# A two-layer MLA, HGRN2 and PEER block: the target tokens x lie by tokens from the end of their first pass on, and parts of the HGRN phase are moved

## Chip, core and metric

The kernel runs on one core of a Trainium2 chip. What is measured is the device time of the launch in microseconds: of the execution, from the first instruction to the last. A time before is the median of three runs; the profile is that of one more execution.

## What is computed

Two layers work on 256 target tokens x and 256 context tokens, each token with 1024 features, all in fp32. Layer 0 has an MLA and convolution mixer and a PEER feed-forward, for both kinds of tokens. Layer 1 has an HGRN2 mixer and a PEER feed-forward, for x alone. The result is a root-mean-square norm of x. Cut to what the change touches:

```python
x = x + mod[5] * peer_ffn(modulate(rms_norm(x, norm2_g[0]), mod[3], mod[4]), ...)   # layer 0
h = modulate(rms_norm(x, norm1_g[1]), mod[0], mod[1])                               # layer 1
q, zf, zb, i, g = split(h @ w_in)
o = gla_chunked(q, kf, i, lf, sc_f) + flip(gla_chunked(flip(q), flip(kb), ...))     # 8 heads, 4 chunks of 64
y = (rms_norm(o, 1) * norm_g * silu(g)) @ w_out
x = x + mod[2] * y
h2 = modulate(rms_norm(x, norm2_g[1]), mod[3], mod[4])
x = x + mod[5] * peer_ffn(h2, ...)
return rms_norm(x, final_norm_g)

def peer_ffn(h, ...):      # 8 heads, 128 keys a half, the best 16 of 16 x 16 sums: 16 experts of 16384
    act = gelu(einsum('nd,nhkd->nhk', h, u[eidx]))
    return einsum('nhk,nhkd->nd', softmax(top_s) * act, v[eidx])
```

## The kernel before

Activations lie transposed: `xT` has the 128 features of a tile on the partitions, 8 tiles, and the 512 tokens (x, then context) in the free dimension. Weights come as tiles of 512 KB through `wring`, a ring of four: `load_tile` (L99) lets SyncE issue tile g once the product of tile g-4 is counted in `acc_ready`. `lin` (L95) lists the products in order, `lin_matmuls` (L118) and `lin_evac` (L133) run one.

**The PEER phase** (`peer_phase`, L891) is a program by picks. A step is one head for one block of 128 tokens, it has 16 picks, and a pick is one expert per token: GpSimd gathers for it 128 rows of u and v (8 KB each, 1 MB) into one of eight slots `uv` (L1032), VectorE forms the dot products with the tokens' own rows `H2` (L1340), ScalarE gelu, gate and a diagonal (L1170, L1174, L1180), and TensorE adds diagonal times v into `pY` (L1120), two matmuls of 128x512, each of them two records. A slot is free for gather n+8 once pick n is added. In layer 0 the picks k = 4, 9 and 13 of each step from pick 148 on are added by VectorE into `Y` instead (`on_vector`, L926; L1301). The choice of experts for a step (`topk`, L1201) runs on VectorE two steps ahead. Layer 0 has 512 picks: 16 steps for the context tokens, then 16 for x. Layer 1 has 256. Beside the picks of layer 0 two companions work, `TargetMixer` (layer 0's mixer for x) and `ContextStates` (the HGRN states that the context leaves, the last of them at pick 503); each has methods `sync`, `tensor`, `scalar` and `vector` that are called with the pick's number.

**The end of a block of tokens**: `take` (L1282) copies `pY` (L1290), or adds it to `Y` (L1288), `turn_back` (L1069) transposes it to features in two halves through `pt` (L1077), and `residual` (L1309) adds it, times the modulation, into `xT` (L1316). For the first block of a pass this runs beside the next step's picks (k = 8 to 15), for the last block behind the last pick.

**A norm** (`norm_phase`, L164) is a phase of its own, with barriers about it: ScalarE squares 8 tiles (L196), TensorE sums them over the features with a matrix of ones (L207), VectorE and ScalarE form the inverse root for all columns (L213, L198, L215), VectorE multiplies (L218), and both apply gain and shift (L186, L190). It runs ahead of the HGRN phase (`n1`), ahead of layer 1's PEER phase (`np1`) and for the result (`nf`), which is then stored in one transfer of 1 MB (L285).

**The HGRN phase** (`hgrn_phase`, L2095) has three parts. First the products `hg_zz` (16 tiles, gates), values of features 0 to 511 with `wi`, `hg_qg` (16 tiles, queries and output gate), and the other values. SyncE issues `wi` (2 MB, L2143) ahead of tile 4 of `hg_zz`. GpSimd issues eight tiles of the modulation's weights `ada_w` (2 MB each, L2154), two at once and each further one when the one before last is used up; VectorE multiplies them in between the gates of the 16 half heads (L2229, L2230, `products(3 * i, 3 * i + 3)`), and TensorE sums four columns of partial results (`turn(n)`, L2158) after tiles 5, 8, 11 and 14 of `hg_zz` and 0, 4 and 8 of `hg_qg`, and the last time behind the values.

```python
L2227  for i in range(2 * HEADS):
L2228      lin_done(dve, 5, i + 1)
L2229      chain(v.tensor_scalar(F[:, i], F[:, i], room[:, i:i + 1], low[:, i:i + 1], ALU.mult, ALU.add))
L2230      chain(v.tensor_scalar(KK[:, i], F[:, i], -1.0, 1.0, ALU.mult, ALU.add))
L2231      products(3 * i, 3 * i + 3)
```

Second the recurrence, head by head: exponentials on ScalarE two heads ahead (L2274), their products on VectorE (L2308) and GpSimd (L2270), key transposes, intra-chunk scores, states and output on TensorE, and ScalarE's copy of a head's output (L2301), which releases the output bank for the next. Third the output: squares of all heads (L2423), their column sums (L2453), an inverse root, 16 diagonals (L2437) that TensorE spreads over the features (L2460), the products with norm, gain and gate (L2441, L2444), then `hg_out` (8 tiles, each the features of one output tile, L127), which waits for all eight heads, and a residual per tile (L230). Behind it stand `np1` and the opening of `peer_phase`: queries and scores of head 0 for 256 tokens, the tokens' own rows (L1087, L1151), head 1; then `topk` and the first gather. SyncE loads the 12 query tiles that the ring does not hold into `held` at the start of this phase (L1009).

## Time and profile before

| | |
|---|---|
| three runs | 2677.03, 2678.91, 2681.13 us; median 2678.91 |
| the profiled execution | 2672.03 us, its span 2669.9 us |
| TensorE busy | 2259.8 us, 85% |
| VectorE busy | 1813.7 us, 68% |
| ScalarE busy | 1113.0 us, 42% |
| GpSimd busy | 895.4 us, 34% |
| DMA | 949.67 MB, mean 356 GB/s over the span |
| mean granted clock of TensorE | 0.958 of full speed |

The times of rows are microseconds from the start of the span. PE is TensorE's matmuls, PEld its weight loads, DVE VectorE, ACT ScalarE, POOL GpSimd, SP SyncE. A timeline row merges instructions of one line that follow each other ("x16"); its second number reaches from the start of the first to the end of the last. In brackets stands how long the engine had been idle and what ended that.

### The profile page before, as it was taken

The numbers are of one execution on the slowest core, as the hardware profiler recorded it, in microseconds if no ns is written. First come the engines' busy times: TensorE is split into PE (matmuls) and PEld (weight loads), VectorE is DVE, ScalarE is ACT, GpSimd is POOL, SyncE is SP. The second block draws the span as 40 slices with busy tenths as digits, with TensorE's granted clock in tenths as the row PEclk, the third lists the DMA queues.
The fourth block names the chain that finished last, engine by engine and source line by source line (L and its number), as shares of the span: only waits on it lengthen the run. The fifth ranks groups of instructions, "written<-read, shape, count | busy, mean of one in ns | idle before, by whom it ended". The sixth has DMA issues, their size and how long they took to land. (4 is left out here: it accounts for less than half of the span.)

```text
span 2669.9 us, 24714 instructions
## 1 busy us (share of the span) xinstructions
PE 2259.8 (85%) x7264; PEld 1239.9 (46%) x7264; DVE 1813.7 (68%) x4325; ACT 1113.0 (42%) x3039; POOL 895.4 (34%) x802
## 2 busy tenths in 40 slices
PE   7999799999887988888888877699787888888776
PEld 3776445543453324444444443477663333333222
DVE  3745988876668666868687867571637666666655
ACT  1352558754535343434343434211314444444443
POOL 0000444443344434444444444000204444444431
PEclk8999899999899999899999999899998999999999
DMA  8423999999999999999999999584049999999995
GB/s 324 158 87 105 367 418 419 406 421 420 397 418 420 420 420 419 415 419 414 418 412 420 414 417 411 210 308 136 1 163 409 427 427 427 426 427 427 426 427 230
DMA packets 146247, 949.67 MB, mean 356 GB/s; under 512 B 16448, under 2 KB 22080, under 8 KB 43712
## 3 DMA queue, kind: packets, MB, share of 16 engines
q0 software_dynamic: 112608, 834.72, 75.4%
q1 hardware_dynamic: 33504, 113.37, 11.6%
q8 instruction: 58, 0.95, 0.1%
q14 instruction: 77, 0.63, 0.1%
HBM read 946.98 MB, written 1.05 MB: 355 GB/s over the span
## 5 line engine op out<-in xcount | busy, mean ns | idle before, releaser
L1120 PE MATMUL pY<-uv,diag 128*128 128x512 f32 x2796 | 1369.5, 625 | 306.3 <-ACT diag L1180 304.5
L1032 POOL DMA_INDIRECT uv<-uv_dram,idx x768 | 869.9, 1133 | 1321.3 <-PE pY L1120 826.0
L1340 DVE SCALAR_TENSOR_TENSOR uv<-uv,H 128x1024 f32<-128x1024 f32 x768 | 940.3, 1224 | 534.1 <-DMA uv<-uv_dram,idx 532.0
L1120 PEld LDWEIGHTS pY<-uv,diag 128*128 128x128 f32 x2796 | 511.9, 195 | 1043.6 <-ACT diag L1180 572.0
L1170 ACT ACTIVATE gelu<-dots 128x1 f32<-128x1 f32 x768 | 155.1, 202 | 979.7 <-DVE uv L1340 978.6
L1180 ACT ACTIVATE diag<-cst,coef 128x128 f32<-128x128 f32 x699 | 280.6, 401 | 65.7 <-ACT coef L1174 1.9
L1174 ACT ACTIVATE coef<-gelu,gate 128x1 f32<-128x1 f32 x768 | 226.3, 295 | 28.1 <-ACT gelu L1170 0.4
L1055 PE MATMUL pqs<-h2T,wring 128*128 128x256 f32 x576 | 133.5, 387 | 11.3 <-PEq L168 7.4
L1055 PEld LDWEIGHTS pqs<-h2T,wring 128*128 128x128 f32 x576 | 111.8, 195 | 39.4 <-issue 25.1
L127 PE MATMUL plh<-h1T,wring 128*128 128x256 f32 x512 | 117.5, 391 | 11.8 <-PEq L168 7.4
L127 PEld LDWEIGHTS plh<-h1T,wring 128*128 128x128 f32 x512 | 99.9, 197 | 27.1 <-issue 8.2
L461 PE MATMUL f_pl<-h,wring 128*128 128x256 f32 x384 | 95.8, 394 | 1.3 <-ACT h L619 1.3
L1170 ACT ACT_TABLE_LOAD x72 | 92.4, 1283 | 1.3
L1301 DVE SCALAR_TENSOR_TENSOR Y<-uv,coef,Y 128x1024 f32<-128x1024 f32 x65 | 83.3, 1281 | 0.0
L461 PEld LDWEIGHTS f_pl<-h,wring 128*128 128x128 f32 x384 | 73.4, 198 | 11.4 <-issue 1.8
L1907 PE MATMUL side<-h2T,arena 128*128 128x256 f32 x256 | 63.4, 392 | 0.0
L1340 DVE DVE_READ_ACCUMULATOR uv<-uv,H 128x1 f32 x768 | 63.3, 82 | 0.0
L1907 PEld LDWEIGHTS side<-h2T,arena 128*128 128x128 f32 x256 | 51.2, 200 | 21.1 <-issue 15.2
L1144 ACT ACT_TABLE_LOAD x46 | 59.0, 1283 | 0.8
L1758 DVE SCALAR_TENSOR_TENSOR arena<-arena,convw 128x256 f32<-128x256 f32 x120 | 56.8, 473 | 0.3
L798 DVE SCALAR_TENSOR_TENSOR convc<-gatedc,convw,convc 128x256 f32<-128x256 f32 x120 | 48.9, 482 | 0.0
L752 DVE SCALAR_TENSOR_TENSOR mod_part<-aw,scT,mod_part 128x512 f32<-128x512 f32 x70 | 47.0, 745 | 0.4
...
## 6 DMA issues: line engine op xcount, KB each, us to landing
...
uv<-uv_dram,idx POOLq DMA_INDIRECT x768, 14.8
...
```

The source lines that it names most:

```text
L127: last = nc.tensor.matmul(psum[:, j, 0:n_cols], wring[:, j, k * P:(k + 1) * P], rhs(k), start=(k == 0), stop=(k == KT - 1))
L461: last = mm(pl[g // 2 % 2][:, i % 2, :], wring[:, g % RING, k * P:(k + 1) * P], rhs, start=(k == 0 and (i % 2 == 0 or not (seq == 2 and i ...
L1032: nc.gpsimd.indirect_dma_start(out=uv[:, n % SLOTS, :], out_offset=None, in_=t[f"uv{l}"], in_offset=bass.IndirectOffsetOnAxis(ap=idx[:, s ...
L1055: last = nc.tensor.matmul(pq[:, i, :], w[:, k * P:(k + 1) * P], hT[:, k, own:own + T], start=(k == 0), stop=(k == KT - 1))
L1120: last = nc.tensor.matmul(pY[:, b, half * 512:(half + 1) * 512], diag[:, multiplied(n) % DIAGS, :], uv[:, n % SLOTS, D + half * 512:D + (h ...
L1144: nc.scalar.activation(gate[:, s % KEPT, :], gate[:, s % KEPT, :], ACT.Exp, bias=nmax[:, s:s + 1], accum_out=den[:, s:s + 1]).then_inc(s_e ...
L1170: nc.scalar.activation(gelu[:, r:r + 1], dots[:, s % 2, k:k + 1], ACT.Gelu).then_inc(s_gelu, 1)
L1174: nc.scalar.activation(coef[:, r:r + 1], gelu[:, r:r + 1], ACT.Copy, scale=gate[:, s % KEPT, k:k + 1]).then_inc(s_coef, 1)
L1180: nc.scalar.activation(diag[:, m % DIAGS, :], ident, ACT.Copy, scale=coef[:, r:r + 1]).then_inc(s_diag, 1)
L1301: last = v.scalar_tensor_tensor(out=to, in0=row, scalar=coef[:, r:r + 1], in1=to, op0=ALU.mult, op1=ALU.add)
L1340: v.scalar_tensor_tensor(out=uv[:, j, 0:D], in0=uv[:, j, 0:D], scalar=1.0, in1=H2[:, own, :], op0=ALU.mult, op1=ALU.mult, accum_out=dots[: ...
L1907: last = mm(to, self.ring[:, i % 3, k * P:(k + 1) * P], self.hT[:, k, :], start=(k == 0), stop=(k == KT - 1), skip_group_check=True)
```

## The change

All parts stand in one change.

- x by tokens. At the end of x's PEER pass in layer 0 `RowFinish` takes the place of `take`, `turn_back` and `residual` for x, and of the norm `n1`. Rows of x and of the modulation are made ahead, beside the picks. For each block of 128 tokens VectorE multiplies the sum by the gate and adds x (`RowNorm.sums`), ScalarE squares with a row sum, the inverse root is one number per token, and TensorE turns the block to features by matmuls with the diagonal of these numbers, so that it is normed on the way (`turn`); gain and shift are applied on the way out of PSUM. Block 0 runs beside the last picks, from pick 499 on, block 1 behind the last. `xT` holds x by tokens from there on.
- The last two steps of layer 0 add nothing on VectorE, and what it had added before is folded into the rows of x in the step before the last.
- The same class ends layer 1: it makes the result by rows and stores it in four transfers of 256 KB; the norm `nf` and the one store are gone. The host lays the output out accordingly.
- The HGRN output and the opening of layer 1 are one program inside the PEER phase (`RowOutput`): the product with `hg_out` has tokens on its output rows and sums over heads, tile by tile (each tile now holds the rows of one head), so it can begin when the first head is gated; block 0 is finished, normed, turned and asked for its experts ahead of block 1. `np1` is gone. The squares of the recurrence's output are made per head, ahead of the output's copy.
- The HGRN phase: SyncE issues tiles 4 to 9 of `hg_zz` ahead of `wi`; GpSimd waits for the fourth tile's product before it issues `ada_w`; its memsets, the exponentials and products of heads 0 and 1 stand in the first part, ahead of the last values' copies; `turn(7)` stands ahead of the last values.
- `Y` and one `hT` are made once for the whole kernel.

The diff's core (indentation reduced):

```diff
   s, k = divmod(n, TOPK)
-  return l == 0 and n >= VECTOR_FROM and k in (4, 9, 13)
+  return l == 0 and n >= VECTOR_FROM and k in (4, 9, 13) and s < steps - 2
...
       residual(done, 1)
-   take(steps - 1)
-   residual(steps - 1, 0)
-   residual(steps - 1, 1)
+   for n in TAIL:
+    for side in sides:
+     side.vector(dve, n)
+class RowNorm:
...
+ def sums(self, dve, b):
+  v = self.nc.vector
+  for h in range(2):
+   own = slice(2 * h, 2 * h + 2)
+   v.tensor_tensor(self.temp(b)[:, own], self.src(b)[:, own], self.gate[:, own], ALU.mult).then_inc(self.prod, 1)
+  for h in range(2):
+   own = slice(2 * h, 2 * h + 2)
+   dve.wait_ge(self.prod, 2 * b + h + 1)
+   v.tensor_tensor(self.out(b)[:, own], self.temp(b)[:, own], self.residual(b)[:, own], ALU.add).then_inc(self.x, 1)
+ def squares(self, act, b):
+  for h in range(2):
+   own = slice(2 * h, 2 * h + 2)
+   act.wait_ge(self.x, 2 * b + h + 1)
+   self.nc.scalar.activation(self.junk(b)[:, own], self.out(b)[:, own], ACT.Square,
+         accum_out=self.ss[:, 2 * b + h:2 * b + h + 1]).then_inc(self.sq, 1)
+ def mean(self, dve, b):
+  v, ms = self.nc.vector, self.ms[:, b:b + 1]
+  dve.wait_ge(self.sq, 2 * b + 2)
+  v.tensor_tensor(ms, self.ss[:, 2 * b:2 * b + 1], self.ss[:, 2 * b + 1:2 * b + 2], ALU.add).then_inc(self.mean_ready, 1)
+  dve.wait_ge(self.mean_ready, 2 * b + 1)
+  v.tensor_scalar(ms, ms, 1.0 / D, EPS, ALU.mult, ALU.add).then_inc(self.mean_ready, 1)
+ def root(self, act, b):
+  act.wait_ge(self.mean_ready, 2 * b + 2)
+  self.nc.scalar.activation(self.ms[:, b:b + 1], self.ms[:, b:b + 1], ACT.Sqrt).then_inc(self.root_ready, 1)
+ def inverse(self, dve, b):
+  dve.wait_ge(self.root_ready, b + 1)
+  self.nc.vector.reciprocal(self.ms[:, b:b + 1], self.ms[:, b:b + 1]).then_inc(self.inv, 1)
+  dve.wait_ge(self.inv, b + 1)
+ def diagonal(self, dve, b):
+  self.nc.vector.tensor_scalar(self.spread(b), self.ident, self.ms[:, b:b + 1], None, ALU.mult).then_inc(self.diag, 1)
+ def turn(self, pe, b, banks):
+  pe.wait_ge(self.diag, b + 1)
+  for k in range(KT):
+   last = self.nc.tensor.matmul(banks[k // 4][:, k % 4 * P:(k % 4 + 1) * P], self.out_cols(b, k), self.spread(b),
+          start=True, stop=True)
+   if k % 4 == 3:
+    last.then_inc(self.turned, 1)
+ def affine(self, eng, b, k, banks, to, gain, shift):
+  eng.wait_ge(self.turned, 2 * b + k // 4 + 1)
+  own = banks[k // 4][:, k % 4 * P:(k % 4 + 1) * P]
+  if eng is self.nc.scalar:
+   eng.activation(to, own, ACT.Identity, scale=gain, bias=shift).then_inc(self.h_act, 1)
+  else:
+   eng.tensor_scalar(to, own, gain, shift, ALU.mult, ALU.add).then_inc(self.h_dve, 1)
+def feature_rows(nc, bank, half, column, ident):
+ for k in range(4):
+  last = nc.tensor.matmul(bank[:, k * P:(k + 1) * P], column(4 * half + k).broadcast_to([P, P]), ident,
+        start=True, stop=True)
+ return last
+class RowFinish:
+ TAIL = 12
+ SUM, SQUARE, MEAN, ROOT, INVERSE, TURN, AFFINE = 0, 1, 2, 2, 3, 4, 5
+ OPEN, GATE, ADDED = 317, 467, (2, 4, 6, 8)
...
+ def begins(self, b):
+  return self.picks - TOPK + 3 if b == 0 else self.picks
...
+ def tensor(self, pe, n):
...
+      pe.wait_ge(self.g_copied, 1)
+     feature_rows(nc, self.banks[0], half, self.column(0), self.ident).then_inc(self.g_rows, 1)
+   for b in range(2):
+    if n == self.begins(b) + self.TURN:
+     if b == 0:
+      pe.wait_ge(self.context.k_copied, 8)
+      pe.wait_ge(self.context.st, 16)
+     else:
+      pe.wait_ge(row.h_act, 4)
+      pe.wait_ge(row.h_dve, 4)
+     row.turn(pe, b, self.banks)
...
+   if n == self.begins(b) + self.SQUARE:
+    row.squares(act, b)
+   if n == self.begins(b) + self.ROOT:
+    row.root(act, b)
+   if self.l == 0 and n == self.begins(b) + self.AFFINE:
+    for k in range(4):
+     row.affine(act, b, k, self.banks, *self.into(b, k))
...
+  for b in range(2):
+   if n == self.begins(b) + self.SUM:
+    dve.wait_ge(self.s_pick, self.own_picks[b])
+    if b == 0:
+     dve.wait_ge(self.g_copied, 2 if self.l == 0 else 4)
+     if self.l == 0:
+      dve.wait_ge(self.copied, 4)
+      if self.added:
+       dve.wait_ge(self.folded, 4)
+    row.sums(dve, b)
+   if n == self.begins(b) + self.MEAN:
+    row.mean(dve, b)
+   if n == self.begins(b) + self.INVERSE:
+    row.inverse(dve, b)
+    if self.l == 0:
+     row.diagonal(dve, b)
+    else:
+     for h in range(2):
+      own = slice(2 * h, 2 * h + 2)
+      v.scalar_tensor_tensor(out=row.temp(b)[:, own], in0=row.out(b)[:, own], scalar=row.ms[:, b:b + 1],
+           in1=self.rows["gain"][:, own], op0=ALU.mult, op1=ALU.mult).then_inc(self.y, 1)
+   if self.l == 0 and n == self.begins(b) + self.AFFINE:
+    for k in range(4, KT):
+     row.affine(dve, b, k, self.banks, *self.into(b, k))
+ def sync(self, sp, n):
+  if self.l == 1:
+   for b in range(2):
+    for h in range(2):
+     if n == self.begins(b) + self.INVERSE:
+      sp.wait_ge(self.y, 2 * b + h + 1)
+      sp.dma_start(self.final[1][:, b, h * 512:(h + 1) * 512],
+         self.row.temp(b)[:, 2 * h:2 * h + 2].rearrange("p j n -> p (j n)")).then_inc(self.final[2], 16)
+class RowOutput:
...
+ def sync_out(self, sp):
+  for i in range(RING, KT):
+   self.load_tile(sp, "hg_out", i, self.out_first + i)
+  for i in range(RING):
+   self.load_tile(sp, "peer_q1", i, self.q_first + i)
...
+  for half in range(2):
+   last = feature_rows(nc, self.pY[:, 0, half * 512:(half + 1) * 512], half, lambda k: self.modT[:, 1, 2, k, 0:1], self.ident)
+  last.then_inc(self.g_rows, 1)
+  for n in range(HEADS * M):
+   last = mm(self.pt[:, n:n + 1], self.sq[:, n // M, (n % M) * P:(n % M + 1) * P], self.ones[:, 0:1], start=True, stop=True)
+  last.then_inc(self.r_sum, 1)
+  def wide(q):
+   pe.wait_ge(self.r_diag, q + 1)
+   if q >= 3:
+    pe.wait_ge(self.r_on, q - 2)
+   mm(self.wide[q % 3], self.ones[:], self.diag[:, 2 * M * q:2 * M * (q + 1)].rearrange("p m n -> p (m n)"),
+   start=True, stop=True).then_inc(self.r_wide, 1)
+  def product(k, blocks):
+   g = self.out_first + k
+   pe.wait_ge(self.w_loaded[g % RING], 16 * (g // RING + 1))
+   pe.wait_ge(self.r_gated, k + 1)
+   if k == 0:
+    pe.wait_ge(self.g_copied, 1)
+   for b in blocks:
+    for half in range(2):
+     last = mm(self.pY[:, b, half * 512:(half + 1) * 512], self.O[:, k, b * P:(b + 1) * P],
+       self.wring[:, g % RING, half * 512:(half + 1) * 512], start=(k == 0), stop=(k == KT - 1),
+       skip_group_check=True)
+   if blocks[-1] == 1:
+    last.then_inc(self.acc_ready, 1)
+   elif k == KT - 1:
+    last.then_inc(self.b0_out, 1)
+  wide(0)
+  wide(1)
+  wide(2)
+  product(0, (0, 1))
+  product(1, (0, 1))
+  wide(3)
+  product(2, (0, 1))
+  product(3, (0, 1))
+  for b in range(2):
+   for k in range(4, KT):
+    product(k, (b,))
+  def queries(b, bank):
+   for i in range(2):
+    g = self.q_first + i
+    pe.wait_ge(self.w_loaded[g % RING], 16 * (g // RING + 1))
+    for k in range(KT):
+     if i == 0 and b == 0:
+      pe.wait_ge(row.h_act if k < 4 else row.h_dve, k % 4 + 1)
+     if i == 0 and b == 1:
+      pe.wait_ge(row.h_act, 4 + k + 1)
+     last = mm(bank[:, i, 0:P], self.wring[:, g % RING, k * P:(k + 1) * P], self.hT[:, k, b * P:(b + 1) * P],
+       start=(k == 0), stop=(k == KT - 1))
+    if b == 1:
+     last.then_inc(self.acc_ready, 1)
+   if b == 0:
+    last.then_inc(self.q_done, 1)
+  def scores(b):
+   pe.wait_ge(self.q_copied, b + 1)
+   pe.wait_ge(self.s_keys[0], 16)
+   if b == 1:
+    pe.wait_ge(self.s_first, 1)
+   for i in range(2):
+    last = mm(self.psc[:, b, i, :], self.qT[:, i, b * P:(b + 1) * P], self.keys[:, 0, i, :], start=True, stop=True)
+   last.then_inc(self.s_done if b == 0 else self.s_sc, 1)
+  def rows(b):
+   pe.wait_ge(row.x, 2 * b + 2)
+   for half in range(2):
+    for k in range(4):
+     last = nc.tensor.transpose(self.pY[:, b, (4 * half + k) * P:(4 * half + k + 1) * P],
+           self.hT[:, 4 * half + k, b * P:(b + 1) * P], self.ident)
+   last.then_inc(self.t_done, 1)
...
+  a, row = self.nc.scalar, self.row
+  act.wait_ge(self.g_rows, 1)
+  a.copy(self.gate_row, self.pY[:, 0, :]).then_inc(self.g_copied, 1)
+  act.wait_ge(self.r_dve, 1)
+  a.activation(self.rs, self.rs, ACT.Sqrt).then_inc(self.r_root, 1)
+  row.squares(act, 0)
+  row.root(act, 0)
+  for k in range(4):
...
+   dve.wait_ge(self.r_on, q + 1)
+   for h in (2 * q, 2 * q + 1):
+    v.scalar_tensor_tensor(out=self.O[:, h], in0=self.on[:, h], scalar=self.vecs[:, self.hg_gain + h:self.hg_gain + h + 1],
+         in1=self.gated[:, h], op0=ALU.mult, op1=ALU.mult).then_inc(self.r_gated, 1)
+  dve.wait_ge(self.b0_out, 1)
+  dve.wait_ge(self.g_copied, 1)
+  row.sums(dve, 0)
+  row.mean(dve, 0)
+  row.inverse(dve, 0)
+  row.diagonal(dve, 0)
+  for k in range(4, KT):
+   row.affine(dve, 0, k, (self.pt, self.b[0]), *self.into(0, k))
+  dve.wait_ge(self.acc_ready, self.out_first + KT)
+  row.sums(dve, 1)
+  dve.wait_ge(row.x, 4)
+  dve.sem_inc(self.acc_free, KT)
...
     def _(sp):
+     for i in range(RING, 10):
+      load_tile(sp, "hg_zz", i, first[5] + i)
      sp.dma_start(wi[:], t["hg_i"][:, :, 0:512]).then_inc(s_wi, 16)
-     lin_loads(sp, 5)
+     for i in range(10, 16):
+      load_tile(sp, "hg_zz", i, first[5] + i)
+     lin_ahead(sp, 5)
      sp.wait_ge(s_i, 2)
      sp.dma_start(wi[:], t["hg_i"][:, :, 512:D]).then_inc(s_wi, 16)
      lin_loads(sp, 6)
     @block.gpsimd
     def _(pool):
+     for e in two:
+      for d in two:
+       nc.gpsimd.memset(AM[e][d][:], 0.0).then_inc(s["zero"], 1)
+     pool.wait_ge(acc_ready, first[5] + RING)
      for n, g in enumerate(LATER):
       if n >= 2:
        pool.wait_ge(m_used, n - 1)
       pool.dma_start(aw[:, n % 2, :], t["ada_w"][g]).then_inc(m_loaded[n % 2], 16)
+     for h in range(AHEAD):
+      inward_keys(pool, h)
+     lin_matmuls(pe, 6, pl, lambda k: hT[:, k, 0:T], T, after=lambda i: turn(i // 4 + 4) if i in (0, 4, 8) else None)
+     turn(7)
      values(1)
-     turn(7)
...
-     nc.scalar.activation(QG[:, HEADS:], QG[:, HEADS:], ACT.Silu)
+     nc.scalar.activation(gated, gated, ACT.Silu)
+     act.wait_ge(s_lb, 4 * HEADS + 6)
+     for h in range(AHEAD):
+      exponentials(act, h)
+     for d in two:
+      nc.scalar.activation(dec[:, halves[d], :].rearrange("p h c -> p (h c)").unsqueeze(2),
+           last_col(d), ACT.Exp).then_inc(s["dec"], 1)
...
        act.wait_ge(s["o"], h)
+       nc.scalar.activation(sq[:, h - 1], pO[:, 0:T], ACT.Square)
        nc.scalar.copy(OT[:, h - 1], pO[:, 0:T]).then_inc(s["oc"], 1)
...
```

## Rows read from the trace of the kernel before

**Rows 1.** The page, part 2: busy tenths in 40 slices of 66.7 us.
```profile
DMA  8423999999999999999999999584049999999995
```

**Rows 2.** Windows by stage: stretch, its length, busy PE, PEld, DVE, ACT, POOL; PEclk; DMA; GB/s.
```profile
990.00:1688.00 698.00, 575.25 (x1700) 296.02 (x1700) 524.75 (x1233) 289.98 (x844) 299.67 (x251) 0.95 1.00 413
1688.00:2002.00 314.00, 266.02 (x1329) 217.04 (x1330) 149.84 (x303) 66.12 (x136) 19.28 (x21) 0.92 0.44 156
2002.00:2645.00 643.00, 539.52 (x1277) 224.14 (x1277) 430.44 (x1063) 279.75 (x843) 268.92 (x256) 0.98 1.00 419
2645.00:2669.90 24.90, 9.21 (x28) 6.02 (x28) 9.57 (x23) 6.29 (x14) 0.00 (x0) 0.74 0.10 42
```

**Rows 3.** Groups by line: out<-in, shape, count | busy us, mean ns | idle before.
```profile
L127 PE MATMUL plo<-QG,wring 128*128 128x256 f32 x128 | 27.9, 380 | 2.8 <-DVE QG L2444 2.8
...
L2441 DVE TENSOR_TENSOR on<-pB,QG 128x512 f32<-128x512 f32 x4 | 2.8, 688 | 0.5 <-PE pB L2460 0.4
```

**Rows 4.** Timeline, end of layer 0: start, us, engine, line, op [idle before].
```profile
1693.19 1.23 DVE L1288 TENSOR_TENSOR Y<-pY,Y 128x1024 f32<-128x1024 f32 x1 [1.56 <-PE pY L1120]
...
1697.11 1.13 DVE L1316 SCALAR_TENSOR_TENSOR xT<-pt,modT,xT 128x128 f32<-128x128 f32 x4 [0.81 <-PE pt L1077]
1699.56 2.56 ACT L196 ACTIVATE n_sqb<-xT 128x256 f32<-128x256 f32 x8 [9.11 <-PEq L71]
...
1702.14 1.28 ACT L198 ACT_TABLE_LOAD   x1
...
1713.37 16.46 PE L127 MATMUL plh<-h1T,wring 128*128 128x256 f32 x64 [7.38 <-PEq L168]
```

**Rows 5.** The ada_w issues' landing, and the timeline of the first HGRN product.
```profile
DMA to landing us min/median/max: 8.4/9.7/17.6
...
1725.55 0.49 DVE L2217 TENSOR_SCALAR h_part<-arena,scT 128x512 f32<-128x512 f32 x1 [4.88 <-DMA arena<-ada_w_dram]
...
1733.00 0.49 DVE L2217 TENSOR_SCALAR h_part<-arena,scT 128x512 f32<-128x512 f32 x1
...
1734.23 6.14 PE L127 MATMUL plh<-h1T,wring 128*128 128x256 f32 x17 [4.40 <-DMA wring<-hg_zz_dram]
...
1744.26 10.61 PE L127 MATMUL plh<-h1T,wring 128*128 128x256 f32 x48
```

**Rows 6.** Timeline, last values copy and start and end of the recurrence.
```profile
1867.15 0.59 ACT L2194 COPY VI<-pi 128x512 f32<-128x512 f32 x1 [6.28 <-PE pi L2174]
...
1874.26 1.12 PE L2352 MATMUL pK<-cst,F 128*128 128x128 f32 x4 [6.36 <-DVE qin L2313]
...
1925.46 0.37 ACT L2301 COPY QG<-pOh 128x256 f32<-128x256 f32 x1 [2.98 <-PE pOh L2370]
```

**Rows 7.** Timeline, HGRN output up to its first product.
```profile
1926.80 4.21 PE L2453 MATMUL pR<-ones,osq 128*128 128x1 f32 x32 [1.38 <-ACT osq L2423]
...
1932.54 5.75 PE L2460 MATMUL pB<-odiag,ones 128*128 128x512 f32 x8 [1.53 <-DVE odiag L2437]
...
1935.38 0.88 DVE L2444 SCALAR_TENSOR_TENSOR QG<-on,vecs,QG 128x256 f32<-128x256 f32 x2
...
1941.05 5.23 PE L127 MATMUL plo<-QG,wring 128*128 128x256 f32 x23 [2.76 <-DVE QG L2444]
```

**Rows 8.** Timeline, start of layer 1 up to its first gather.
```profile
1982.30 6.48 SPq L1009 DMA_DIRECT2D held<-peer_q_dram  x12
...
1990.77 1.16 PE L1065 MATMUL pqs<-keys,qT 128*128 128x128 f32 x8 [0.74 <-ACT qT L1134]
...
1992.58 0.29 DVE L1209 MAX8 sv<-S 128x8 f32<-128x128 f32 x1 [11.70 <-ACT S L1140]
...
2001.97 1.01 POOL L1032 DMA_INDIRECT uv<-uv_dram,idx  x1 [92.27 <-DVE idx L1268]
```

**Rows 9.** Timeline, behind the last pick: its copy, and the store of the result.
```profile
2647.01 1.23 DVE L1290 COPY Y<-pY 128x1024 f32<-128x1024 f32 x1 [2.10 <-PE pY L1120]
...
2665.71 0.35 SPq L285 DMA_DIRECT2D out_dram<-yT  x1
```

562 lines of the change are left out of this document (321 added, 241 removed).

## The prediction

> **What bounds the kernel now.** I read the slices of the page first [rows 1]: the DMA engines are full through nearly all of the two stretches of gathers and stand low at the front and in slices 26 to 30. The stages say the same [rows 2]: from 990 to 1688 us and from 2002 to 2645 us the DMA share is 1.00 at 413 and 419 GB/s, and 256 gathers fill the last of them, 643 / 256 = 2.51 us each. No engine is busy for all of it (TensorE 575 of 698 us), so work added to or taken from these two stretches costs nothing as long as the gathers keep coming. What can be won lies where no gather flows: the 314 us from the last gathers of layer 0 to the first of layer 1, and the 24.9 us behind the last one. The change touches both, so I follow the chain of each, from the timeline.
>
> **Prices.** An elementwise product or sum of 128x512 takes VectorE 0.69 us; the whole output product of the HGRN block takes TensorE 27.9 us [rows 3]. A 128x256 square costs ScalarE 2.56 / 8 = 0.32 us [rows 4], so one of 128x512 about 0.65, with its sum's readout 0.85. A small fp32 matmul of 128x128 is two records, and eight records take 1.16 us, 0.145 each [rows 8]; four transposes took 1.12 us where TensorE had just been idle [rows 6], so I take 0.22 for a record there.
>
> **Part 1, end of layer 0 (from the last pick to h1).** Before: 1693.19 (last pick done) to 1713.37 (first HGRN matmul), 20.2 us [rows 4]: a copy, two turn-backs, a barrier of 1.3 (1698.24 to 1699.56), and a whole norm over 256 tokens. After, block 0 is done beside the last picks. Of block 1 there stay: two products and two sums 4 x 0.69 = 2.8; the last square 0.85; the square root's table 1.3, beside which the mean is formed; root, reciprocal and diagonal, three small ones with a semaphore each, 0.7; eight matmuls with the diagonal, 16 x 0.22 = 3.5; the last affines about 1.2; the barrier 1.3. Sum 11.7, gain **8.5**. Bounds: 7, if each semaphore costs more than I think, and 10.5, if TensorE stays at its full clock (16 x 0.145). The page "ScalarE: Activation LUTs" of the Trainium skill (What ACT_TABLE_LOAD costs) puts 1.4 us of drain to each table load; here the load of 1.28 starts at 1702.14, 0.02 behind the last square, so the trace does not agree, and by the page the gain here and in part 5 would be 1.4 less each.
>
> What moves under the last 16 picks: sums, squares, root and affines of block 0, in both layers, two table loads more each, in layer 0 four folds of Y, and six picks back from VectorE to TensorE. TensorE waits at pick 503 for the last context state, then turns for 2.3 us. I cost all this at nothing: the cover is the transfers, whose landing is several gathers behind their issue. If the cover fails, each us late on the last pick is a us on the end.
>
> **Part 2, loads of the first HGRN product.** Before, the 2 MB of wi and two ada_w tiles of 2 MB start together and tile 4 of hg_zz comes behind them: TensorE waits 4.4 us at 1734.23, and its next 17 records take 6.14 where 48 take 10.61 later on, 2.4 more than at full clock [rows 5]. After, hg_zz goes first and this stall, 6.8 us, is gone. But POOL now waits for the fourth tile before it issues the first ada_w tile. Before, that tile landed at 1725.55, 12.2 us after the first matmul (at S), and VectorE's eight products with it, between the gates of three heads, took until 1733.0, 7.45 us. TensorE asks for them at turn(0), behind tile 5. Now: the first four tiles end at S+16.5 [rows 4], the landing takes 9.7 (8.4 to 17.6 in the row), hence S+26, and VectorE, which is held in order by this wait, is done at S+33.5. TensorE reaches turn(0) two tiles of 3.5 later, at S+23.4, waits 10 us, turns for 1 and comes out at the low clock, as it did at 1734. Tile 6 starts at S+34.5 against 1744.26 - 1713.37 = S+30.9 before, and runs 2.4 slower: a **loss of 6**. Bounds: nothing lost, if the loads land in 8.4 us, the tile behind the wait is not slow, and neither are the first ones; 9 lost if ring tiles and ada_w share their way badly. A new wait takes the old one's place, and it is longer.
>
> **Part 3, start of the recurrence.** Exponentials of two heads, their products on VectorE and POOL, and POOL's memsets move under the last values matmuls; turn(7) goes ahead of these, so VectorE has its modulation early. Before, the last values copy is at 1867.15 and TensorE's first transpose at 1874.26 [rows 6]. After, it should come right behind the barrier, at about 1869.2: 5.1 us; head 0 meets a VectorE that no longer works on head 1's keys, which I put at 0.9. Against it stands a square per head on ScalarE ahead of the copy that releases the next output, 8 x 0.32 = 2.5. In each head that copy also stands ahead of ScalarE's share in the next, so I charge all eight. Gain **3.5**; bounds 1 and 5.5.
>
> **Part 4, HGRN output to the first gather of layer 1.** Let G be the end of the last copy, 1925.8 [rows 6]. Before: sums of squares ready at 1931.0, first product at 1941.05, done at 1969.0, then barrier, norm, 256-token queries, scores; top-k at 1992.58, first gather at 2001.97 = G+76.2 [rows 7, 8]. After: 0.3 of barrier; eight matmuls that spread the gate, 2.3; the 32 records of column sums 4.2, now not waiting for squares: G+6.8, 1.6 later than before. Three of the four wide matmuls: six of the eight records of 1932.54 and the wait of 1.5 ahead of them, 6.2, while the first heads are gated (first one 4.9 behind the sums). Products start at G+13 and no more wait for all eight heads, 27.6 + 0.9 for the fourth wide one: G+41.4. Block 0's norm lies under block 1's last four products (6.9 us against about 5.3). Behind the products: turn 2.3, four affines 1.0, sums of block 1 2.8, square 0.85, mean and root 0.7 (ScalarE's queue has them ahead of the query copy), copy 0.4, scores 0.6, copy 0.4: 9.0, then top-k up to the first gather as before, 9.4 [rows 8]: G+59.8. Gain **16.3**. The twelve loads of held tiles, issued from 1982.30 on [rows 8], are 6.3 MB, 15 us at 419 GB/s; they now start at about G+42 and end about where the first gather starts; no term. The first dot comes about 1 us later behind that gather, since head 1's queries are late, but eight gathers of 2.5 are under way. Bounds: 11, if the short pieces run at the low clock and the held loads push the gathers; 18.
>
> **Part 5, the tail.** Before: 2647.01 to 2669.9, 22.9 us, of it 4.2 for the one store of 1 MB [rows 9]. After: 2.8 for products and sums, 0.85, table 1.3, 0.7, the last 128x512 by scale and gain 0.7 x 2, and a store of a quarter of a MB: 4.2 less three quarters of 1 MB / 419 GB/s (1.9) = 2.4. Sum 9.5 + 0.3 for the queues; gain **13.1**; bounds 11.5 and 14.
>
> **Sum.** -8.5 + 6 - 3.5 - 16.3 - 13.1 = -35.4. The profiled execution took 2672.03 (its span 2669.9): 2636.6. It lies 6.9 below the median of 2678.91, whose three runs span 4.1; by the median the forecast is 2643.5. All parts at their good bounds give -48, at their bad ones -21.5. About 0.2%, 5 us, is what can be told from no change.
>
> **Rivals.** (a) The moved ada_w loads cost nothing, because they land early or TensorE comes later to turn(0): 2637.5. For it: 8.4 us landings. Against: VectorE's queue, in which tile 0 of ada_w stands ahead of head 1. (b) Chains of small pieces run at the low clock and semaphores add up: parts 4 and 5 win 11 and 11.5, part 3 wins 1, 2653. For it: from 2645 on, where TensorE is busy for 9.2 of 24.9 us, the granted clock averages 0.74 of full speed [rows 2]. The page "TensorE: Matmul & The Clock Gate" of the Trainium skill (Part 1) has the half clock as default after idling, which would make every turn behind a norm slow; by it part 4 gives some 2 us back. Here the trace has both cases, so the sum takes the slow record only in part 1. (c) Slower than before: Y and hT now live through the whole kernel and uv, diag and H2 move, and side work sits between the picks; if this stretches the gathers' pace, the time follows at 768 to one. It decides from 35.4 / 768 = 0.046 us per gather, 2.51 to 2.56; at 0.06 the kernel takes 2690. Against: the share is 1.00 with TensorE, VectorE and ScalarE free for a sixth of the time or more. (d) A gain only in the tail, the rest taken up by new waits: within 0.2% if even that goes.
>
> **How the numbers follow.** The forecast has 0.60, (a) 0.15, (b) 0.17, (c) 0.04, (d) 0.04, half of it no change. Range 2629 to 2660: from all good bounds with 2 us of spread, to all bad bounds with the same. Faster 0.94, same 0.02, slower 0.04.
>
> **What would show it.** First HGRN matmul 11.7 us behind the last pick; TensorE waiting near 10 us at turn(0), VectorE waiting for ada_w before it; first transpose 0.5 behind the values copy; first output product at G+13, first gather at G+60; last store's end within 10 us of the last pick. It is wrong if the gathers' stage is longer than 643 us, or if turn(0) comes without a wait.

## The result, and the profile after

The changed kernel takes 2648.47 us (median of four runs, 2646.92 to 2649.94), the kernel before 2678.55 beside it: 30.1 us less, ratio 0.9885 (95% interval 0.9873 to 0.9897). The forecast was 2643.5, 35.4 less; the measured time lies 5.0 above it, inside the range of 2629 to 2660. The profiled execution of the changed kernel took 2649.94, with a span of 2648.1.

The page of the changed kernel, part 2, has the GB/s of 40 slices of 66.2 us:

```profile
GB/s 327 159 88 102 364 418 419 406 420 419 395 418 419 411 419 415 414 416 411 410 419 403 419 417 413 215 363 184 10 171 414 421 421 420 421 421 421 421 422 297
```

The stages, as windows (same columns as [rows 2]):

```profile
990.00:1688.00 698.00, 585.54 (x1754) 304.38 (x1755) 524.24 (x1239) 300.53 (x864) 296.23 (x251) 0.95 1.01 413
1688.00:1992.00 304.00, 268.28 (x1340) 209.12 (x1338) 148.74 (x322) 69.19 (x156) 24.94 (x28) 0.95 0.47 170
1992.00:2634.00 642.00, 540.03 (x1288) 227.03 (x1288) 421.10 (x1027) 283.82 (x850) 262.21 (x249) 0.98 1.00 416
```

Between the gathers of the two layers PE is about as busy as before (268.3 and 266.0 us) in a shorter stretch. But the last stage of picks, at a DMA share of 1.00 like before, moved 416 GB/s where it had moved 419 [rows 2], and its full slices show 421. In the kernel before these slices show 427 (its page is below, with the control run). That is the surprise of the case.

The timeline of the changed kernel behind the last pick of layer 0, against [rows 4]:

```profile
1697.22 1.29 DVE L1364 TENSOR_TENSOR Y<-pY,hT 128x512 f32<-128x512 f32 x2 [3.13 <-PE pY L1095]
...
1700.49 1.28 ACT L1389 ACT_TABLE_LOAD   x1
...
1702.66 2.05 PE L1405 MATMUL pt<-rest,xT 128*128 128x128 f32 x8 [5.47 <-DVE rest L1399]
1704.50 1.91 PE L1405 MATMUL side<-rest,xT 128*128 128x128 f32 x8
...
1706.45 1.36 DVE L1417 TENSOR_SCALAR hT<-side,gainT,modT 128x128 f32<-128x128 f32 x4 [3.94 <-PE side L1405]
...
1709.43 0.93 PE L127 MATMUL plh<-hT,wring 128*128 128x256 f32 x3 [3.02 <-PEq L71]
```

From the last pick (1697.18) to the first HGRN matmul it is now 12.25 us; it was 20.2. Then the first HGRN product, against [rows 5]:

```profile
1725.47 1.14 POOL L2617 DMA_DIRECT2D arena<-ada_w_dram  x2 [15.17 <-PE plh L127]
...
1734.26 0.49 DVE L2689 TENSOR_SCALAR h_part<-arena,scT 128x512 f32<-128x512 f32 x1 [18.26 <-DMA arena<-ada_w_dram]
...
1741.68 1.86 PE L2627 MATMUL pmh<-ones,h_part 128*128 128x1 f32 x8 [9.60 <-DVEq L2697]
```

GpSimd issues the two loads 16.0 us behind the first matmul, VectorE gets the first at 1734.26, and TensorE stands 9.6 us in front of its first turn. The recurrence and the HGRN output, against [rows 6 to 8]:

```profile
1869.31 0.58 ACT L2659 COPY VI<-pi 128x512 f32<-128x512 f32 x1 [5.74 <-PE pi L2639]
...
1870.20 0.63 PE L2790 MATMUL pK<-cst,F 128*128 128x128 f32 x4 [0.93 <-PEq L2582]
...
1924.53 0.37 ACT L2749 COPY Y<-pOh 128x256 f32<-128x256 f32 x1
...
1930.72 0.17 DVE L1752 TENSOR_SCALAR out_rs<-pt 128x16 f32<-128x16 f32 x1 [11.55 <-PE pt L1614]
...
1936.47 4.03 PE L1634 MATMUL pY<-wring,Y 128*128 128x512 f32 x9
...
1944.20 20.76 PE L1634 MATMUL pY<-wring,Y 128*128 128x512 f32 x48
...
1982.79 1.01 POOL L1004 DMA_INDIRECT uv<-uv_dram,idx  x1 [75.03 <-DVE idx L1253]
```

And the tail, against [rows 9]:

```profile
2638.73 1.29 DVE L1364 TENSOR_TENSOR Y<-pY,hT 128x512 f32<-128x512 f32 x2 [3.13 <-PE pY L1095]
...
2643.73 1.42 DVE L1554 SCALAR_TENSOR_TENSOR Y<-xT,row_means,hT 128x512 f32<-128x512 f32 x2
2644.51 0.99 SPq L1567 DMA_DIRECT2D out_dram<-Y  x2
```

From such rows each profiled execution splits into seven stages: the last pick of layer 0; from it to the first HGRN matmul; to the start of the last values copy (first product); to the end of the last output copy (recurrence); to the first gather of layer 1 (output); to the last pick (picks); to the end (tail). "Before again" and "aligned" are experiments, told below.

| us | before | before again | after | after, aligned | fastest |
|---|---|---|---|---|---|
| last pick of layer 0 at | 1693.2 | 1693.4 | 1697.2 | 1673.0 | 1675.2 |
| finish | 20.2 | 20.7 | 12.3 | 12.3 | 12.3 |
| first product | 153.8 | 154.2 | 159.9 | 160.2 | 148.9 |
| recurrence | 58.7 | 60.3 | 55.6 | 54.1 | 52.5 |
| output | 76.1 | 80.2 | 57.9 | 58.8 | 59.1 |
| picks of layer 1 | 645.0 | 644.4 | 655.9 | 646.6 | 645.6 |
| tail | 22.9 | 23.7 | 9.4 | 9.5 | 9.5 |
| span | 2669.9 | 2676.8 | 2648.1 | 2614.4 | 2602.9 |

The five stages that the forecast costed gave 36.7 us (8.0 - 6.1 + 3.1 + 18.2 + 13.5), near its 35.4. Layer 1's picks took 10.9 back, and in this pair of executions the last pick of layer 0 came 4.0 later.

### The profile page after: what moved, and what is told of

Read it like the earlier page. It is cut to its first block and busy times, and to the rows that moved or that the text cites. A ratio compares the mean times of both kernels' runs of the same rounds, so it can differ in the third digit from the quotient of the medians.

```text
span 2648.1 us, 24794 instructions
## 1 busy us (share of the span) xinstructions
PE 2273.5 (86%) x7320; PEld 1240.8 (47%) x7320; DVE 1797.2 (68%) x4299; ACT 1126.4 (43%) x3077; POOL 895.3 (34%) x802
## 3 DMA queue, kind: packets, MB, share of 16 engines
q1 hardware_dynamic: 33936, 113.37, 11.6%
HBM read 946.98 MB, written 1.05 MB: 358 GB/s over the span
## 5 line engine op out<-in xcount | busy, mean ns | idle before, releaser
L1095 PE MATMUL pY<-uv,diag 128*128 128x512 f32 x2820 | 1386.9, 629 | 292.9 <-ACT diag L1159 289.5
L1095 PEld LDWEIGHTS pY<-uv,diag 128*128 128x128 f32 x2820 | 521.1, 196 | 1035.7 <-ACT diag L1159 542.8
L1027 PE MATMUL pqs<-hT,wring 128*128 128x256 f32 x544 | 125.4, 385 | 4.5 <-PEq L71 3.9
L1027 PEld LDWEIGHTS pqs<-hT,wring 128*128 128x128 f32 x544 | 105.3, 194 | 31.9 <-issue 18.6
L127 PE MATMUL plh<-hT,wring 128*128 128x256 f32 x512 | 116.4, 389 | 3.0 <-PEq L71 3.0
L127 PEld LDWEIGHTS plh<-hT,wring 128*128 128x128 f32 x512 | 99.4, 195 | 17.6 <-issue 3.8
L1286 DVE SCALAR_TENSOR_TENSOR Y<-uv,coef,Y 128x1024 f32<-128x1024 f32 x59 | 75.5, 1280 | 0.0
L2330 PE MATMUL side<-hT,arena 128*128 128x256 f32 x256 | 61.3, 383 | 0.0
L2330 PEld LDWEIGHTS side<-hT,arena 128*128 128x128 f32 x256 | 49.3, 193 | 19.3 <-issue 14.0
L2580 POOL TENSOR_TENSOR kin<-kin,KK 128x512 f32<-128x512 f32 x8 | 12.5, 1562 | 107.6 <-ACT F L2566 107.6
```

What stands on the lines that cost most here:

```text
L127: last = nc.tensor.matmul(psum[:, j, 0:n_cols], wring[:, j, k * P:(k + 1) * P], rhs(k), start=(k == 0), stop=(k == KT - 1))
L1027: last = nc.tensor.matmul(pq[:, i, :], w[:, k * P:(k + 1) * P], hT[:, k, own:own + T], start=(k == 0), stop=(k == KT - 1))
L1095: last = nc.tensor.matmul(pY[:, b, half * 512:(half + 1) * 512], diag[:, multiplied(n) % DIAGS, :], uv[:, n % SLOTS, D + half * 512:D + (h ...
L1286: last = v.scalar_tensor_tensor(out=to, in0=row, scalar=coef[:, r:r + 1], in1=to, op0=ALU.mult, op1=ALU.add)
L2330: last = mm(to, self.ring[:, i % 3, k * P:(k + 1) * P], self.hT[:, k, :], start=(k == 0), stop=(k == KT - 1), skip_group_check=True)
```

## The experiments

"Aligned" means the changed kernel with both gather buffers moved. Its median, 2615.1, is what the later runs are held against. The kernel before ran in each group at 2677.6 to 2679.2, so groups can be compared. A stage's length comes from one profiled execution of each kernel.

**Why layer 1's picks are slower: the buffer's address.** The two kernels issue the same gathers from the same table. What differs is where the buffer `uv1` begins in each partition: byte 80640 before, 88896 after. Layer 0's moved from 142560 to 142624. No view of the profile shows these addresses; the paddings below were worked out from them. First a control, the kernel before unchanged:

> The kernel before once more, unchanged, for the pace of layer 1's 768 picks. In the profiled executions shown, its DMA moved 427 GB/s in the full slices of layer 1 and first gather to last pick took 645.0 us (2001.97 to 2646.96); the changed kernel moved 421 and took 655.9 (1982.79 to 2638.68). Theory P, the pace belongs to the program (where its gather buffer lies in SBUF): 427 again, 645 +- 1. Theory E, the pace is that of the one execution that was profiled: some other rate, 421 to 427, and a stage of 645 to 656 us.

2678.89 us. Its page has the same 427 in layer 1, and the stage took 644.4 us:

```profile
GB/s 326 158 84 116 374 418 419 407 420 421 395 418 420 411 420 420 416 418 411 420 407 420 418 417 407 206 305 115 1 163 398 427 427 427 427 427 427 426 427 230
```

So the pace belongs to the program, not to the execution. Then 64 bytes:

```diff
+        if l == 1:
+            sb("pad1", [P, 16], ctx=c)
         uv = sb(f"uv{l}", [P, SLOTS, 2 * D], ctx=c)
```

> The changed kernel with 64 unused bytes per partition ahead of layer 1's gather buffer, and nothing else. In the kernel before this buffer begins at byte 80640 of each partition, a multiple of 128; in the changed one at 88896, 64 past a multiple; here at 88960, a multiple of 128 again. Layer 0's buffer stays at 32 past a multiple. Theory P (placement sets the rate of the gathers): 427 GB/s in layer 1's full slices in place of 421, first gather to last pick 645 to 647 us, and the time 8 to 11 us under the changed kernel's 2648.5, about 2638 to 2640. Theory E (execution): the same as the changed kernel within 3 us, 421 GB/s.

2646.44 us (2645.10 to 2650.01), 2.0 under the changed kernel and not the 8 to 11 of theory P, which had asked for a multiple of 128. The stage took 655.3 us and the full slices stay at 421:

```profile
GB/s 326 160 88 100 360 418 419 404 419 419 396 418 419 413 420 419 415 417 415 416 418 405 419 415 413 218 361 186 11 172 414 421 421 421 420 421 421 421 422 301
```

A multiple of 128 is not enough. 80640 is a multiple of 256, and 88960 is not. With 48 elements in place of 16 the buffer begins at 89088, which is one:

```diff
-            sb("pad1", [P, 16], ctx=c)
+            sb("pad1", [P, 48], ctx=c)
```

> The changed kernel with 192 unused bytes ahead of layer 1's gather buffer alone, which then begins at byte 89088, a multiple of 256; layer 0's stays at 142624, 32 past a multiple. Theory P: 427 GB/s in layer 1's full slices, first gather to last pick 645 to 647 us in place of 655.9, layer 0 as in the changed kernel, the time 8 to 11 us under 2648.5: 2637 to 2641. If layer 1's placement was not what cost the change its 10.9 us there: within 3 us of 2648.5.

2639.16 us, 9.3 less than the changed kernel; picks of layer 1 646.6 us:

```profile
GB/s 327 160 88 100 337 418 418 404 420 419 396 418 419 419 420 417 416 416 412 416 419 406 419 414 417 237 339 210 26 131 414 427 427 426 426 427 427 427 426 308
```

The rate came back in layer 1 and, as the padding said, only there. Layer 0 had never had it, in either kernel (32 and 224 past a multiple). Both at once:

```diff
+        sb(f"pad{l}", [P, (56, 48)[l]], ctx=c)
         uv = sb(f"uv{l}", [P, SLOTS, 2 * D], ctx=c)
```

> The changed kernel with 224 unused bytes ahead of layer 0's gather buffer and 192 ahead of layer 1's, so that both begin at a multiple of 512 bytes (142848 and 89088). Theory P: layer 1 as with 64 bytes, 427 GB/s and 8 to 11 us less; in layer 0, where full slices show 413 to 420 GB/s with the buffer 32 past a multiple of 64, up to 427 too, which at the same bytes would be worth up to 3% of some 690 us of shared stage, 5 to 20 us more, unless TensorE sets the pace there (575 of 698 us busy). Together 2620 to 2640. Theory E: no difference over 3 us.

2615.14 us, ratio 0.9768 (0.9748 to 0.9787): 33.3 less than the changed kernel, 9 of it from layer 1 and 24 from layer 0, whose best slices now show 425 to 427 where they had 418 to 420:

```profile
GB/s 330 162 89 101 330 425 426 404 426 427 407 425 427 421 426 426 426 426 424 422 422 416 424 425 416 210 365 187 10 168 417 427 427 426 427 427 427 427 427 306
```

And the same for the kernel before, where only `uv0` has to move:

```diff
+        if l == 0:
+            sb("pad0", [P, 8], ctx=c)
         uv = sb(f"uv{l}", [P, SLOTS, 2 * D], ctx=c)
```

> The kernel before with 32 unused bytes ahead of layer 0's gather buffer, which moves it from byte 142560 to 142592 of each partition, a multiple of 256; layer 1's stays at 80640, a multiple of 256 as it is. Theory P (a gather buffer that begins at a multiple of 256 bytes is filled at up to 427 GB/s, one that does not at 421 or less): layer 0's full slices at 425 to 427 in place of 418 to 420, layer 1 unchanged, the time 22 to 30 us less, 2648 to 2656. The change by itself, both kernels placed alike, is then 2615.1 minus this: -34 to -41. Theory Q (the 33 us that both paddings gave in the changed kernel need a multiple of 512, or lie in something else that moved): within 5 us of 2678.

2654.71 us, ratio 0.9919 (0.9897 to 0.9940); the last pick of layer 0 at 1669.4, where the control has 1693.4, and layer 1 as it was:

```profile
GB/s 328 158 88 108 371 426 426 407 427 427 405 426 427 418 426 420 426 425 425 424 413 426 426 424 419 200 301 105 1 184 424 427 426 427 426 427 427 426 425 233
```

Theory Q fell. A padding moves whatever lies behind the gather buffer too, and no run moved that buffer alone; but in both kernels and both layers the rate went with its address, and 64 bytes moved the same neighbours without effect.

The page "DMA: Bandwidth & Descriptors" of the Trainium skill (How a descriptor splits into AXI transactions) has a transfer cut at 256-byte boundaries, with what lies ahead of an unaligned start paid too. It speaks of the bytes that are fetched; here the address that was moved is the target's. The boundary is the one found here, and so far the trace agrees. By its beats of 32 bytes, an estimate, a row of 8 KB would take 2 more on 256 at 64 past the boundary (0.8%) and 4 at 128 past (1.6%); here both give 421 for 427 GB/s, 1.4%.

With both kernels placed alike the change is worth 2615.1 - 2654.7 = -39.6 us. In the changed kernel as it is, about 10 of that (39.6 less 30.1) are lost to layer 1's address.

**What the first product waits for.** GpSimd's wait taken away:

```diff
-                    pool.wait_ge(acc_ready, first[5] + RING)
```

> The changed kernel with GpSimd's wait for the fourth HGRN tile taken away, so that the first two ada_w loads (2 MB each) are issued some 16 us earlier, right behind the four memsets. Theory A (turn(0) behind tile 5 waits 9.6 us for products of a load that was issued at 1725.5, and 5.2 us of it reach the last tile): the wait of the first turn gone, the last gate tile 4 to 5.5 us earlier behind the first HGRN matmul (S+68.4 to S+69.6 for S+73.6), the time 4 to 5.5 us less than the changed kernel's. Rival B (the 4 MB then share the DMA engines with tiles 4 to 7 and these come late): TensorE waits for the fifth to seventh tile by 2 to 6 us, the time within 2 us of the changed kernel's or above.

2643.97 us, 4.5 less, but the stage fell only from 159.9 to 157.7; the rest lies in an earlier last pick of layer 0 (1695.6) and a shorter recurrence (54.0), which both differ from execution to execution. The first turn waits no more; a later tile does, in the timeline of TensorE:

```profile
1730.48 0.95 PE L2626 MATMUL pmh<-ones,h_part 128*128 128x1 f32 x8
...
1753.58 10.04 PE L127 MATMUL plh<-hT,wring 128*128 128x256 f32 x32 [7.34 <-DMA wring<-hg_zz_dram]
```

Rival B expected tiles 5 to 7; it is tile 10, behind the 2 MB of `hg_i` that the change put between tiles 9 and 10. Putting `hg_i` first again, alone (aligned):

```diff
-                    for i in range(RING, 10):
-                        load_tile(sp, "hg_zz", i, first[5] + i)
                     sp.dma_start(wi[:], t["hg_i"][:, :, 0:512]).then_inc(s_wi, 16)
-                    for i in range(10, 16):
-                        load_tile(sp, "hg_zz", i, first[5] + i)
-                    lin_ahead(sp, 5)
+                    lin_loads(sp, 5)
```

> The changed kernel, both buffers at multiples of 512, and the first half of hg_i (2 MB) issued ahead of HGRN tile 4 as in the kernel before, in place of between tiles 9 and 10. Theory A (what the stage lost is the late ada_w loads; hg_i's place only chooses which tile is late): a wait of 4 to 5 us for tile 4 comes back and the turn still waits for what is left of its 9.6, the stage from first HGRN matmul to last values copy 159 to 162 us, the time within 3 us of 2615.1. Rival: the loads ahead of tile 4 hide the ada_w wait entirely and the stage falls to 154 to 155, 5 us less.

2618.84 us (2616.77 to 2626.43), 3.7 above aligned; stage 161.0 for 160.2, and the turn waits as in the changed kernel:

```profile
1721.16 1.86 PE L2624 MATMUL pmh<-ones,h_part 128*128 128x1 f32 x8 [9.63 <-DVEq L2694]
```

No wait for tile 4 came back, unlike my expectation: without the `ada_w` loads beside it `hg_i` lets tile 4 through in time. As long as the turn waits, `hg_i` first gains nothing.

The DMA engines stand still during the finish (aligned, 1677 to 1685: share 0.00), so the loads could go there. GpSimd issues them behind the last pick:

```diff
+                def pool_tail(pool):
+                    pool.wait_ge(s_pick, own_picks[1])
+                    pool.wait_ge(context.st, 16)
+                    for j in range(2):
+                        pool.dma_start(arena[:, 2 * HEADS * P + j * KT * 512:2 * HEADS * P + (j + 1) * KT * 512],
+                                       t["ada_w"][16 + j]).then_inc(aw_loaded[j], 16)
...
-                    pool.wait_ge(acc_ready, first[5] + RING)
-                    for n, g in enumerate(LATER):
+                    for n, g in list(enumerate(LATER))[2:]:
```

> The changed kernel with both gather buffers at multiples of 512 bytes, and the first two ada_w loads (4 MB) issued by GpSimd right behind the last pick of layer 0, in the finish in which the DMA engines stand still (share 0.00 to 0.03 for some 12 us), in place of behind the fourth HGRN tile. Theory A (the 6 us that the stage from the first HGRN matmul to the last values copy lost are the ada_w loads behind the fourth tile): TensorE waits neither for the first turn nor for a tile for more than 2 us, the stage 153.5 to 155.5 us in place of 160.1, the time 4 to 6.5 us under 2615.1, about 2609 to 2611. Rival B (the stage is bound by the bytes that it moves, the wait only turns up elsewhere as in the run without the wait, where TensorE stood 7.3 us for a tile at 1753.6): 157 to 158 us, 2 to 3 us less.

2619.07 us, 3.9 more than aligned. The first product did get shorter, 157.2 for 160.2, with no wait for the turn but 7.25 us for tile 10, as rival B had it. The loads were in by about 1688, at up to 437 GB/s, as the windows show; but the finish grew from 12.3 to 19.1:

```profile
1681.00:1684.00 3.00, 3.00 (x15) 3.00 (x16) 0.00 (x0) 1.07 (x4) 0.00 (x0) 0.50 1.00 426
1684.00:1687.00 3.00, 0.59 (x3) 0.30 (x2) 1.37 (x4) 0.43 (x2) 0.00 (x0) 0.50 1.02 437
1687.00:1690.00 3.00, 0.00 (x0) 0.00 (x0) 0.00 (x0) 0.00 (x0) 0.00 (x0) 0.50 0.17 71
1690.00:1693.00 3.00, 0.00 (x0) 0.00 (x0) 0.00 (x0) 0.00 (x0) 0.00 (x0) 0.50 0.00 0
```

From 1688 to 1694 no engine works and next to nothing is moved; then all engines start within 0.3 us (ScalarE at 1694.28, GpSimd last at 1694.57). That the barrier at the phase's end waits for GpSimd is a guess from this; no record names what it waits for. The same loads from the SP queue, with semaphores of their own:

```diff
+                    sp.wait_ge(s_pick, own_picks[1])
+                    sp.wait_ge(context.st, 16)
+                    for j in range(2):
+                        sp.dma_start(arena[:, 2 * HEADS * P + j * KT * 512:2 * HEADS * P + (j + 1) * KT * 512],
+                                     t["ada_w"][16 + j]).then_inc(aw_loaded[j], 16)
```

> As the fastest kernel so far (2600.5 us), but with the first half of hg_i (2 MB) back between HGRN tiles 9 and 10: the changed kernel, both buffers at multiples of 512, with the first two ada_w loads issued by the SP queue behind the last pick and nothing else. Both causes taken apart: if the late ada_w loads are the whole loss, TensorE waits for nothing over 2 us and the stage from the first HGRN matmul to the last values copy is 149 to 151 us, the time 2600 to 2603. If hg_i's place is a second cause, TensorE stands some 7 us for tile 10 behind it (7.3 us in the two runs whose ada_w loads came early), the stage is 156 to 158 us, the time 2607 to 2610.

2607.94 us, 7.2 less than aligned: finish 11.9, first product 157.6. So what held the phase's end goes with the issue by GpSimd, and not with the transfers. The second cause of the expectation is real, 7.91 us for tile 10:

```profile
1732.20 9.62 PE L127 MATMUL plh<-hT,wring 128*128 128x256 f32 x32 [7.91 <-DMA wring<-hg_zz_dram]
```

With `hg_i` first as well:

> The changed kernel, both buffers at multiples of 512, with the first two ada_w loads issued by the SP queue right behind the last pick of layer 0 (GpSimd's run held the end of the phase back by 7 us, although the 4 MB had landed within 12 us), and the first half of hg_i ahead of tile 4. Theory A: the 4 MB land before the first HGRN matmul or up to 2 us behind it, hg_i within 7 us behind it, no wait of TensorE for a turn, and none over 2 us for a tile: finish 12.2 us as before, stage from the first HGRN matmul to the last values copy 149.5 to 153 us in place of 160.1, the time 7 to 10.5 us under 2615.1: 2605 to 2608. Rival D (the phase's end waits for any transfer in flight, whichever engine issued it): finish 17 to 20 us, and 2610 to 2616. Rival B (tile 4 to 10 late by the bytes): stage 155 to 158, 2610 to 2613.

2600.51 us (2596.65 to 2604.72), ratio 0.9706 (0.9692 to 0.9719), faster than both kernels by 78 and 48 us. The stage is 148.9, and TensorE's timeline has no wait in it:

```profile
1687.44 23.94 PE L127 MATMUL plh<-hT,wring 128*128 128x256 f32 x96 [3.05 <-PEq L71]
1711.22 0.95 PE L2634 MATMUL pmh<-ones,h_part 128*128 128x1 f32 x8
1712.03 10.61 PE L127 MATMUL plh<-hT,wring 128*128 128x256 f32 x48
1722.47 0.95 PE L2634 MATMUL pmh<-ones,h_part 128*128 128x1 f32 x8
```

Two causes stood one behind the other, each some 7 to 10 us of waiting; taking one away showed the other, and `hg_i` first is worth 7.4 us with the early loads and nothing without them.

**The exponentials** of the first two heads put back behind the last values copy (aligned; ScalarE's part is shown, the loops of VectorE and GpSimd go with it):

```diff
-                    act.wait_ge(s_lb, 4 * HEADS + 6)
-                    for h in range(AHEAD):
-                        exponentials(act, h)
...
                     values_evac(1)
...
                 @block.scalar
                 def _(act):
+                    for h in range(AHEAD):
+                        exponentials(act, h)
```

> The changed kernel, buffers at multiples of 512, with HGRN's first two heads' exponentials, decays and their products put back to the start of the recurrence, behind the last values copy. By part 3 of the prediction, without the 0.9 us of the turn and the 2.5 us of the squares: the first transpose of the recurrence 5 to 7 us behind the last values copy in place of 0.9, the time 4.5 to 6 us above 2615.1. Rival: GpSimd and VectorE were late with their own part anyway, 0 to 2 us.

2621.00 us, 5.9 more, inside the expected 4.5 to 6. In its timeline the first transpose comes 6.3 us behind the values copy in place of 0.9:

```profile
1841.79 0.58 ACT L2658 COPY VI<-pi 128x512 f32<-128x512 f32 x1 [6.28 <-PE pi L2638]
1842.64 1.28 ACT L2563 ACT_TABLE_LOAD   x1 [0.27 <-PEq L2583]
...
1848.06 1.12 PE L2788 MATMUL pK<-cst,F 128*128 128x128 f32 x4 [6.31 <-DVE qin L2574]
```

**The cover of block 0** taken away, in both layers:

```diff
-        return self.picks - TOPK + 3 if b == 0 else self.picks
+        return self.picks
```

> The changed kernel, buffers at multiples of 512, with the finish of the first 128 tokens put behind the last pick in both layers, in place of beside the last 16 picks. Theory C (that cover costs next to nothing and is worth its length, as parts 1 and 5 of the prediction have it): finish of layer 0 from 12.2 to some 22 us (two more pairs of products and sums, 5.1 us, and a turn with four affines ahead of the second turn, 5.2), tail from 9.4 to some 16 us (5.1 and 2.8 less the overlap); the pick that ends each layer up to 1 us earlier; in all 14 to 18 us above 2615.1. Rival (the work beside the last picks delays them, as the last gather of layer 0 at +8.2 against +5.5 sixteen picks earlier suggests): the last picks end 3 to 5 us earlier in layer 0, and the total is only 9 to 13.

2619.51 us: only 4.4 more, where both theories had 9 or more. Finish 17.2 (+5.0), tail 10.9 (+1.5), layer 1's picks 645.1 (-1.5, within what aligned kernels differ by), and the last pick of layer 0 at 1673.03 against 1673.05. So the work beside the last picks delays them by nothing that shows, and the rival fell. But the theory's price fell too. The timeline says why:

```profile
1670.46 0.68 DVE L1365 TENSOR_TENSOR Y<-pY,hT 128x512 f32<-128x512 f32 x1
...
1671.06 1.28 DVE L1369 TENSOR_TENSOR xT<-Y,H 128x512 f32<-128x512 f32 x2
...
1673.07 1.29 DVE L1365 TENSOR_TENSOR Y<-pY,hT 128x512 f32<-128x512 f32 x2 [0.73 <-PE pY L1096]
```

VectorE is idle while it waits for the last pick, and block 0's sums fall into that wait even when they are put "behind" it. What remains exposed is the turn with its affines in layer 0, and one output product in layer 1.

## Why the prediction was right, and where it was not

**Part 1.** 12.25 us for a forecast 11.7, gain 8.0 for 8.5. The 16 records of the turn ran at half clock (2.05 and 1.91 us for eight each) as taken. The term for the cover, nothing, held. Layer 0's last pick is 4.0 later than before, but not because of the last 16: the gather that starts at 1544.25 before starts at 1548.66, 4.4 later, already. Nor do the picks of layer 0 get slower by the change. Counted from layer 0's first gather, the last pick comes after 1396.5 to 1399.5 us in the seven aligned executions of the changed kernel and after 1398.0 in the aligned kernel before. With the buffer unaligned it takes 1419.0 and 1421.4 us in the two of the kernel before and 1421.1 to 1424.3 in the four of the changed one, and the pair compared here has the shortest and the longest. That first gather starts at 271.4 to 274.2 us in three executions of the kernel before and at 272.2 to 276.7 in eleven of the changed one; whether the change moves it by a us or two stays open.

**Part 2.** Forecast a wait of 10 at the first turn and tile 6 at S+34.5; measured 9.6 and S+34.0 (1743.40), and the stage 6.1 longer for a forecast 6. The 6.1 is made up a little otherwise: the last gate tile ends 5.2 later behind the first matmul (3.1 by the wait and 2.1 by the slow records behind it, 12.72 us for 48 in place of 10.61), and 0.9 is turn(7), which now stands ahead of the last values matmuls and for which I charged nothing. What I did not see is that the place of `hg_i` had its own wait in store.

**Part 3.** Gain 3.1 for 3.5, but by two errors that cancel. The start gained 6.2 (7.1 to 0.9), as forecast (5.1 and 0.9), and the exponentials put back cost it again. The 2.5 us for the squares ahead of each copy do not show: from the first transpose to the last copy's end the fastest kernel needs 51.6 us with the squares, the kernel before 51.6 without them, though its clock was at 0.77 for the first 10, so that some of the 2.5 may hide there. The changed kernel's 54.7 goes with the clock: it was granted 0.83 from 1880 to 1900, where the fastest kernel had 1.00 from 1837 to 1867 (the last section has more of this). So a charge of 2.5 that doesn't show stood against 3.1 that I had not foreseen, and that the sum came out is luck.

**Part 4.** Column sums at G+5.8 (6.8 forecast), products from G+11.6 (13) to G+40.1 (41.4), first gather G+57.9 (59.8). Gain 18.2 for 16.3. The turn behind the norm ran at full clock here (8 records in 1.05 us at 1964.80), so rival (b), the low clock in all small pieces, fell. TensorE was busy for 19.2 of the 20 us from 1960 on, so this was no turn behind idling; the one in part 1 was, 5.47 us idle ahead of it, and it ran at 0.50. The held loads pushed nothing that shows: layer 1's first slice of gathers has 414 GB/s for 409 before.

**Part 5.** 9.4 us for 9.8. The page "ScalarE: Activation LUTs" of the Trainium skill (What ACT_TABLE_LOAD costs) puts a drain to a table load. The trace again shows none: the load starts at 1700.49, 0.02 behind the last readout, and ends 0.02 before the root.

**The step that failed**, though the time came out in the range, is the pace of the gathers, which the sum left as it was. It stands in the prediction as rival (c), which I gave 0.04, and my reason against it was: "the share is 1.00 with TensorE, VectorE and ScalarE free for a sixth of the time or more". The share was full in both kernels, but a full share does not fix how many bytes go through. (c) had the right fact in it ("uv, diag and H2 move") and the wrong mechanism, work between the picks. In layer 1 the pace went from 645.0 / 256 = 2.52 to 655.9 / 256 = 2.56 us per gather, the very figure it named, on 256 gathers of 768. That cost 10.9 us. The prediction's own sign of being wrong, a gathers' stage over 643 us, came true by this (655.9, where the same measure gives 645.0 before). The parts that I did cost came out 1.3 better in the profiled pair.

The rest of the gap is the choice of reference. The profiled execution of before was 6.5 us below the median; the control, at the median, has its longer stages in the output (80.2 for 76.1) and the recurrence (60.3 for 58.7). Against the control the costed stages gave 44.0 us, so the change of -30.1 is not a forecast of 35 with 5 missing. In this pair it is 44 gained, 11.5 lost in layer 1 by the address, and 3.8 by a later last pick of layer 0, most of it no more than executions differ by. That the median came within 5 us of the forecast, with 11 us overlooked, is in part luck.
